# The third norm and the routing on the scaled residual: where a token's factor is put

## What is computed

```python
x = x + jnp.einsum('bsd,de->bse', merged, w_out[l])
h = rms_norm(x, g_ffn[l])          # x * rsqrt(mean(x*x, -1) + EPS) * g_ffn
...
logits = jnp.einsum('bsd,de->bse', h, w_router)
top_val, top_idx = lax.top_k(logits, TOP_K)
top_w = jax.nn.softmax(top_val, axis=-1)
for e in range(N_EXPERTS):
    out = out + gates[..., e:e + 1] * swiglu(h, w1[e], w3[e], w2[e])
```

## Time and profile before

| | us |
|---|---|
| time, median of 3 runs | 1642.52 (1641.66 to 1648.16) |
| profiled execution, its time | 1649.6 |
| profiled execution, its span | 1647.8 |
| PE busy | 1613.0 (98%) |
| DVE busy | 1280.3 (78%) |
| ACT busy | 1040.6 (63%) |

### The profile page before, as it was taken

One profiled execution on the slowest core, in us unless ns is written; L12 is line 12 of the kernel. 1 busy time (PEld: TensorE's weight loads), 2 busy tenths in 40 slices (PEclk: granted clock), 3 DMA queues, 4 the chain that ended last, 5 costly groups with the idle time before them and its releaser, 6 DMA issues.

```text
span 1647.8 us, 23908 instructions
## 1 busy us (share of the span) xinstructions
PE 1613.0 (98%) x9544; PEld 1420.8 (86%) x9544; DVE 1280.3 (78%) x1103; ACT 1040.6 (63%) x914; POOL 15.6 (1%) x16
## 2 busy tenths in 40 slices
PE   7999989999899998999999999999999999999998
PEld 6999989999899997888888888888888888888887
DVE  5985763445697566987988987987987987987986
ACT  5545443544554625777777777777777777777774
POOL 0000100000000010000000000000000000000000
PEclk9999999999999997999999999999999999999999
DMA  8543545555354451999999999999999999999994
GB/s 291 166 150 131 173 133 182 180 194 187 124 159 145 137 179 60 366 367 338 366 367 339 365 366 338 365 365 338 366 366 338 365 366 338 365 366 339 364 366 177
DMA packets 182147, 452.56 MB, mean 275 GB/s; under 512 B 6992, under 2 KB 80720, under 8 KB 181968
## 3 DMA queue, kind: packets, MB, share of 16 engines
q1 hardware_dynamic: 182096, 451.82, 76.3%
HBM read 450.74 MB, written 1.05 MB: 274 GB/s over the span
## 4 chain that ended last, share of the span: by engine, by line
PE 97%; DVE 2%; ACT 0%; issue 0%; DMA 0%; DVEq 0%; ACTq 0%
PE bank L293 30%; PE bank L294 29%; PE bank L295 29%; PE bank L1347 2%; PE bank L1368 1%; PE bank L1389 1%; PE bank L1084 1%; DVE h_full L655 1%; PE bank L1201 1%; DVE rinv L645 0%; PE bank L1192 0%; PE bank L1185 0%; PE bank L1135 0%; DVE w_low L283 0%; PE bank L1184 0%; DVE h_low L650 0%
## 5 line engine op out<-in xcount | busy, mean ns | idle before, releaser
L283 DVE TENSOR_TENSOR w_low<-raw,w_high 128x2048 fp32r<-128x2048 f32 x427 | 959.0, 2292 | 129.3 <-ACT w_high L279 129.0
L279 ACT ACTIVATE w_high<-raw 128x2048 fp32r<-128x2048 f32 x427 | 803.3, 1918 | 134.1 <-DMA raw<-exp_w 132.2
L293 PE MATMUL bank<-w_high,hg_high 128*128 128x512 f32 x896 | 352.9, 394 | 0.7 <-issue 0.7
L294 PE MATMUL bank<-w_low,hg_high 128*128 128x512 f32 x896 | 350.1, 391 | 0.0
L295 PE MATMUL bank<-w_high,hg_low 128*128 128x512 f32 x896 | 350.0, 391 | 0.0
L293 PE MATMUL bank<-h_high,w_high 128*128 128x256 f32 x1056 | 301.9, 286 | 5.6 <-DVE h_low L650 4.8
L295 PE MATMUL bank<-h_high,w_low 128*128 128x256 f32 x1056 | 295.5, 280 | 0.0
L294 PE MATMUL bank<-h_low,w_high 128*128 128x256 f32 x1056 | 295.5, 280 | 0.0
L293 PEld LDWEIGHTS bank<-h_high,w_high 128*128 128x128 f32 x1056 | 201.1, 190 | 12.3 <-issue 10.7
L294 PEld LDWEIGHTS bank<-h_low,w_high 128*128 128x128 f32 x1056 | 199.8, 189 | 1.6 <-issue 1.4
L293 PEld LDWEIGHTS bank<-w_high,hg_high 128*128 128x128 f32 x896 | 168.9, 189 | 36.0 <-issue 0.9
(11 more groups left out here) (250 smaller groups left out, 1525.9 us busy)
## 6 DMA issues: line engine op xcount, KB each, us to landing
raw<-exp_w SPq DMA_DIRECT2D x336, 1024.0 KB, 5.1
raw<-w_in SPq DMA_DIRECT2D x42, 1024.0 KB, 5.2
raw<-ffn_w SPq DMA_DIRECT2D x33, 1024.0 KB, 5.3
raw<-w_out SPq DMA_DIRECT2D x8, 1024.0 KB, 5.0
raw<-w_br_attn SPq DMA_DIRECT2D x4, 1024.0 KB, 5.1
raw<-w_br_pool SPq DMA_DIRECT2D x2, 1024.0 KB, 4.7
raw<-w_br_conv SPq DMA_DIRECT2D x2, 1024.0 KB, 5.5
cst<-consts SPq DMA_DIRECT2D x1, 1280.0 KB, 13.5
```

What stands on the lines that cost most here:

```text
L279: nc.scalar.activation(wh[c % RING][:], raw[c % RING][:], ACT.Copy).then_inc(s["high_done"], 1)
L283: nc.vector.tensor_tensor(wl[c % RING][:], raw[c % RING][:], wh[c % RING][:].bitcast(F32), ALU.subtract).then_inc(s["split_done"], 1)
L293: pe.matmul(dst, lh, rh, start=start and i == 0, stop=False)
L294: pe.matmul(dst, lh, rl, start=False, stop=False)
```

## The change

Only the norm ahead of the experts is changed, in layer 1. The residual is scaled by g_ffn alone, without the norm's factor, as its blocks become ready: ACT writes the high part `y_high`, squares x, and writes a full copy to `gate` (`x_scaled`); DVE writes the low part `y_low` (`x_scaled_low`). The router's logits are made from these, PE turns the full copy into rows by token, and the factor of a token, now one number in its partition, is put on the logits and on the rows as they are copied out (`scale=rtok`). The sum of squares is made for it with a single column of ones (`token_sums`, L1377), so that it lands by token in a partition. Three splits of expert weights on ACT and DVE move from the routing into the four steps of the residual, three clearing writes move from DVE to GpSimd, and the exponential moves behind the four `gather_out`. The core of the diff:

```diff
             def experts():   # ScalarE, and in mixer() ahead of it
-                squares(2 * l + 1, 0)
-                squares(2 * l + 1, 1)
...
+                else:
+                    for m in range(4):
+                        x_scaled(m)
+                        if m < 3:
+                            split_high(act, MOE0 + m)
...
+            def x_scaled(m):
+                x_ready(act, 3, m)
+                for k in (2 * m, 2 * m + 1):
+                    ins = nc.scalar.activation(yH[:, k, :], xT[:, k, :], ACT.Copy, scale=A(1, A_GFFN + k))
+                ins.then_inc(s["xg_high"], 1)
+                squares(3, m)
+                for k in (2 * m, 2 * m + 1):
+                    ins = nc.scalar.activation(xgf[:, k, :], xT[:, k, :], ACT.Copy, scale=A(1, A_GFFN + k))
+                ins.then_inc(s["xg_full"], 1)
...
-                norm(3)
-                split_high(act, MOE0)
-                split_high(act, MOE0 + 1)
...
+                act.wait_ge(s["norm_stats"], 4)
+                for t in range(TT):
+                    ins = nc.scalar.activation(root2[:, t:t + 1], bank[(3, 6)[t]][:, 0:1], ACT.Sqrt, bias=A(0, A_EPS),
+                                               scale=1.0 / D)
+                ins.then_inc(s["norm_root"], 1)
+                act.wait_ge(s["norm_step"], 4)
+                for f, (t, half_) in enumerate(GROUPS):
+                    act.wait_ge(s["xg_turned"], f + 1)
+                    nc.scalar.activation(htH[:, t, 512 * half_:512 * half_ + 512], bank[XG_BANKS[f]][:], ACT.Copy,
+                                         scale=rtok[:, t:t + 1]).then_inc(s["ht_high"], 1)
...
             # VectorE
-                residual(33)
-                residual(34)
...
+                for m in range(4):
+                    residual(33 + m)
+                    if l == 0 and m in (1, 2):
+                        split_low(dve, b + MIX_PIECES + m - 1)
+                    elif l:
+                        if m < 3:
+                            split_low(dve, MOE0 + m)
+                        x_scaled_low(m)
...
+            def ht_low(f):
+                t, half_ = GROUPS[f]
+                cols = slice(512 * half_, 512 * half_ + 512)
+                dve.wait_ge(s["ht_high"], f + 1)
+                nc.vector.scalar_tensor_tensor(out=htL[:, t, cols], in0=bank[XG_BANKS[f]][:], scalar=rtok[:, t:t + 1],
+                                               in1=htH[:, t, cols].bitcast(F32), op0=ALU.mult,
+                                               op1=ALU.subtract).then_inc(s["ht_low"], 1)
...
             # TensorE
+                def token_sums(m):
+                    pe.wait_ge(s["squares"], 12 + m + 1)
+                    for k in (2 * m, 2 * m + 1):
+                        for t in range(TT):
+                            ins = pe.matmul(bank[(3, 6)[t]][:, 0:1], hf[:, k, t * P:t * P + P], ones[:, 0:1],
+                                            start=k == 0, stop=k == KC - 1)
...
+                for k in range(6):
+                    logits(k)
+                for m in range(3):
+                    token_sums(m)
+                for f in range(2):
+                    pe.wait_ge(s["xg_full"], 2)
+                    turn_group(xgf, XG_BANKS[f], f, "xg_turned")
+                logits(6)
+                logits(7).then_inc(s["f_raw"], 1)
+                token_sums(3).then_inc(s["norm_stats"], 1)
+                for f in range(2, 4):
+                    pe.wait_ge(s["xg_full"], 4)
+                    turn_group(xgf, XG_BANKS[f], f, "xg_turned")
+                small_turn(7, 0, 3, "r_logits")
```

More of the change, by code:

```diff
@@ L537, in experts @@
             def experts():
-                norm(3)
-                split_high(act, MOE0)
-                split_high(act, MOE0 + 1)
[L541 to L551, removed]
+                act.wait_ge(s["norm_stats"], 4)
[8 more added lines that the diff above has]
+                                         scale=rtok[:, t:t + 1]).then_inc(s["ht_high"], 1)
+                for f, (t, half_) in enumerate(GROUPS):
+                    act.wait_ge(s["x_turned"], f + 1)
+                    nc.scalar.activation(xacc[:, t, 512 * half_:512 * half_ + 512], bank[X_BANKS[f]][:],
+                                         ACT.Copy).then_inc(s["x_copied"], 1)
                 def gather_out(g, count):
@@ L575, in experts @@
                     gather_out(g, 0)
+                act.wait_ge(s["r_lg"], 1)
+                nc.scalar.activation(wt[:, 1, :], wt[:, 0, :], ACT.Exp).then_inc(s["r_exp"], 1)
                 def job(j):
@@ L660, in norm, with x_scaled_low @@
                 low(3)
+            def x_scaled_low(m):
+                dve.wait_ge(s["xg_high"], m + 1)
+                for k in (2 * m, 2 * m + 1):
+                    ins = nc.vector.scalar_tensor_tensor(
+                        out=yL[:, k, :], in0=xT[:, k, :], scalar=A(1, A_GFFN + k), in1=yH[:, k, :].bitcast(F32),
+                        op0=ALU.mult, op1=ALU.subtract)
+                ins.then_inc(s["xg_low"], 1)
             def mixer(l):
@@ L1320, in experts, with logits @@
             def experts():
-                small_h(bank[7][:, S:2 * S], 64, 3)
-                for f in range(12):
-                    src = (hH, hL, xT)[f // 4]
-                    if f >= 7:
-                        pe.wait_ge(s["fill_act"], f - 6)
-                    if f == 4:
-                        small_turn(7, 0, 3, "r_logits")
-                    t, half_ = f % 4 // 2, f % 2
-                    for k in range(4):
-                        a = src[:, 4 * half_ + k, t * P:t * P + P]
-                        ins = pe.transpose(bank[f % 7][:, k * P:k * P + P], a if f >= 8 else a.bitcast(F32), ident)
-                    ins.then_inc(s["fill"], 1)
+                def logits(k):
+                    if k % 2 == 0:
+                        pe.wait_ge(s["xg_low"], k // 2 + 1)
+                    at = 64 + 8 * k
+                    return products(pe, bank[7][:, S:2 * S], [
+                        (wfH[:, at:at + P], wfL[:, at:at + P], yH[:, k, :], yL[:, k, :])], start=k == 0, stop=k == KC - 1)
@@ new lines, in token_sums, with turn_group @@
+                def token_sums(m):
+                    pe.wait_ge(s["squares"], 12 + m + 1)
+                    for k in (2 * m, 2 * m + 1):
+                        for t in range(TT):
+                            ins = pe.matmul(bank[(3, 6)[t]][:, 0:1], hf[:, k, t * P:t * P + P], ones[:, 0:1],
+                                            start=k == 0, stop=k == KC - 1)
+                    return ins
+                def turn_group(src, b, f, name):
+                    t, half_ = GROUPS[f]
+                    for k in range(4):
+                        ins = pe.transpose(bank[b][:, k * P:k * P + P], src[:, 4 * half_ + k, t * P:t * P + P], ident)
+                    ins.then_inc(s[name], 1)
@@ L1333, in experts @@
+                small_turn(7, 0, 3, "r_logits")
+                pe.wait_ge(s["norm_root"], 4)
+                for f in range(2):
+                    turn_group(xT, X_BANKS[f], f, "x_turned")
                 pe.wait_ge(s["r_pick"], 1)
```

72 lines of the change are left out of this document (42 added, 30 removed).

## The result

| | changed kernel | kernel before |
|---|---|---|
| time, median (range), us | 1651.51 (1647.75 to 1659.68), 20 runs | 1642.25 (1636.78 to 1649.19), 20 runs |
| profiled execution, its time | 1648.27 | 1649.6 |
| its span | 1646.5 | 1647.8 |
| mean granted clock in it | 0.987 | 0.988 |

The medians differ by 9.3 us. The ratio of changed to before, an estimate over all the runs and not the quotient of the two medians, is 1.0053, slower by 0.53%, with a 95% interval of 1.004 to 1.0066. The interval lies on both sides of the 0.5% that the prediction took as its bound.

The account below looks back on a forecast made before the run. PE holds 97% of the chain, and the change lies in the stretch before job 0. Residual round trips and a half-clock backlog start job 0 9.1 us later: 1642.5 + 9 = 1651.5 us, range 1641.5 to 1655.

Parts of the forecast that it names:

- The circle: Layer 1's four residuals: each waits for a round trip through ACT and DVE, 7.7 us instead of PE's 6.3.
- The clearing writes on GpSimd: At 605.7 to about 608, while DVE stands idle waiting for ACT's w_high1; costed at nothing.
- The backlog behind the last low part: PE's logits, sums and turned rows from 629.65, at half clock to 643.2; DVE takes the logits 8.1 us later.
- The one-column entry: Sums of squares on PE: 0.217 us per entry at half clock, bounds 0.11 and 0.217.
- Half clock throughout: PE from the backlog until into job 0 stays at 1.2 GHz; the forecast case, chance 0.75.
- rival 1: Clock returns in the backlog by 633, drops again before the gathers: +2.5 us, 1645; chance 0.13.
- the prediction's own sign of being wrong: PE's clock at 1.00 between 633 and 657, or a residual following its unit on PE within a microsecond.
- The exponential and the fourth split: Exponential behind the last `gather_out`: split ready at 667.8, needed by PE at 668.0, so PE waits below 1 us.
- The sum: Job 0 and all behind it move by +9.1 us; against the median, 1642.5 + 9 = 1651.5.
- Rival 2: Clock full from the backlog into job 0, PE waits for the fourth split: -1.3 us, 1641; chance 0.07.
- Rival 3: Residuals come at PE's pace, the round trip not binding; job 0 starts near 633: -15 us, 1627.5; chance 0.03.
- The size against 0.5%: Same means within 8.2 us, 1634.3 to 1650.7; chances: slower 0.53, same 0.43, faster 0.04.

Follow-up runs that it names:

- a0_same: The changed kernel run again with no edit: median 1654.38 us over 6 runs, ratio 1.0057 to the kernel before.
- a1: The changed kernel with DVE's split of each expert piece one residual later, behind that step's low parts: 1637.32 us, ratio 0.9961 to before.
- a3: The changed kernel with sums of squares and the first two groups of turned rows issued between the logits on PE: 1647.55 us, ratio 1.0022 to before.
- a6: The changed kernel with late DVE splits, exponential ahead of `gather_out`, and turned logits ahead of the last two groups of turned rows: 1629.86 us, ratio 0.9921 to before.
- a2: The changed kernel with the exponential put back ahead of the four `gather_out` on ACT: 1650.96 us, ratio 1.0033 to before.
- a5: The changed kernel with both the late DVE splits and the exponential ahead of the four `gather_out`: 1634.43 us, ratio 0.9959 to before.
- a4: The changed kernel with the exponential first and 30 plus 54 unread products filling PE's waits between logits: 1646.69 us, ratio 1.0011 to before.
- a7: The same kernel as a6, unchanged, on another occasion: 1631.8 us over 6 runs, ratio 0.9936 to before.

## Why the prediction was right, step by step

The forecast was 1651.5 us and the median is 1651.51. The agreement to 0.01 us is luck: the same kernel gives two kinds of executions some 4 us apart, each with or without 7 us of a slower dense loop, and the median falls among them; with the six runs of a0_same it is 1652.3. The circle and its size are no luck.

- **The circle.** Forecast: residuals 9.1, 7.7 and 7.7 us apart, each behind a w_low that waits for ACT's w_high. Measured: 9.04, 7.78 and 7.77, behind waits of 5.62, 4.10 and 4.09 us. Shown as the cause by a1, in which the edit of one order on DVE takes 14 us off.
- **The clearing writes on GpSimd.** They were costed at nothing, and ran from 598.55 to 601.01 in after, while DVE had no work until 604.05. No residual or low part waited for them.
- **The backlog behind the last low part.** Confirmed by a3 (shorter by what goes elsewhere, 3.7 to 5 us). The one-column entry, which no row of before showed, was taken at 0.217 us between bounds of 0.11 and 0.217, and took 0.205 at half clock: 0.012 too much each, 0.4 us over 32. One addition in the working is off by 0.15 us: eight transposes of 1.75 from 647.7 end at 649.45, not 649.3.
- **The clock.** Half clock throughout is what a0_same's profile shows, and there scaling is 0.1 us, the gathers 0.3 and job 0 0.1 us from the forecast. The first profile goes part of the way of rival 1: the clock came back within the backlog and was gone again 0.7 us into the gathers (639.9). But it came back at +35, where that rival had it at +27.7 (633 on the times of before): all 24 of the first entries ran at half clock (4.91 us), and scaling came at +36.80, 1.2 us ahead of the forecast's +37.99, where the rival had +33.1. It loses 5.8 us and not the rival's 2.5. On the times of before the clock was at 1.00 from 640.3 to 647.2, so the prediction's own sign of being wrong, a clock of 1.00 between 633 and 657, shows for 7 of these 24 us in this execution. So the step that was wrong is the weight of "I take half clock until into job 0": that is one of two common outcomes, ten of 26 by their mean clock, and was given 0.75; a return in the backlog was given 0.13, with too early a point.
- **The exponential and the fourth split.** Forecast: they fit by 0.2 us, PE waits less than 1. PE waited 0.79 us in after and 0.65 in a0_same, for the clock came back 3.6 and 3.9 us into job 0, where the sum had 6.1, so that PE was through with its 36 products sooner. That a sooner start would be worth less for it was right too: 2.50 us in a1.
- **The sum.** +9.1 was forecast for job 0 and all behind it; +9.15 at the combine in a0_same, +5.8 in after. Set against the before executions that most of its runs are like (about 1642), the times of the two kinds without the slower dense loop, 1648 and 1651.4 to 1654.4, are 6 and 9.5 to 12.5 more; a0_same's has 2 us more ahead of the changed stretch too (600.00 against 598.01).
- **The rivals.** Rival 2 (full clock throughout) and rival 3 (no circle) did not occur. Rival 3 as a mechanism is a1 and a6: with the circle taken out the kernel is faster than before, by 5 to 13 us, less than the 15 of the rival. The last low part was ready at +17.0 in both (614.47 + 0.88 in a1), where the rival had +14.8; the clock fell in the backlog all the same; and in a1 PE waited for the fourth split.
- **The size against 0.5%.** 9.3 us against the bound of 8.2, with an interval on both sides of it: as close as the chances 0.43 and 0.53 had it.

What stays open: why the clock returns 35 us behind residual 33 in one execution and only at +55 in another, with the same instructions in front of it. The Trainium skill ("TensorE: Matmul & The Clock Gate", Part 1: The HAM clock gate) says that the number of slow matmuls at a start differs from run to run of one kernel; the two profiles of the same kernel agree. Open too is what the exponential's place is worth in time (a2, a5), and why the dense loop has two paces.

## What to carry to other kernels

Where an engine works its stream in order, add up the whole trip round two engines before work is put into the gaps of a step: 5.4 us of it under a pace of 6.3 left the time of this kernel as it was, 7.8 us turned a gain of 5 us into a loss of 9. A split that feeds something much later belongs behind the instructions for which the other engine waits, one step late; that single order turned 0.5% slower into 0.4% faster. And PE's waits were paid twice here, in themselves and in the low clock behind them (3.6 us in a4). Price such a backlog at half clock: even with work at full rate right up to it, the clock fell within it in a1 and a4 to a7.

## What the runs showed of the hardware

Two things about TensorE's clock, and one about the dense loop. First, the clock fell while PE had no wait at all. In a1 PE was busy for all of 614 to 618 us (windows), in products of 256 columns until 613, then one-column sums (613.08 to 615.8) and eight turned blocks:

```profile
614.00:616.00 2.00, 2.00 (x20) 2.00 (x20) 0.99 (x4) 1.76 (x5) 0.00 (x0) 1.00 0.76 313
616.00:618.00 2.00, 2.00 (x12) 2.00 (x11) 0.00 (x0) 0.00 (x0) 0.00 (x0) 0.54 0.00 0
```

The same in a4, behind 10 us of busy products, a wait of 0.3 us and the same sums:

```profile
626.00:628.00 2.00, 2.00 (x16) 2.00 (x17) 0.00 (x0) 0.00 (x0) 0.00 (x0) 0.78 0.00 0
```

It also fell so in a5 (0.62 over 616 to 617, then 0.50), a6 (622 to 624: 0.92, then 0.50) and a7 (614 to 616: 1.00, then 0.50). In before it held through the turned rows of 631.3 to 637 and the rank's start, behind logits, so turned rows alone are not enough to explain it; the five kernels in which it fell so have the 24 one-column entries just ahead. Whether these are the cause was not tried by itself. A one-column float32 matmul costs two entries of 0.114 us at full clock and 0.205 at half, 4.91 us for the 24 entries of twelve matmuls that give one number per token.

Second, being busy did not bring the clock back. In a0_same PE was busy without a break from 625 to 639.8 us, in logits, one-column sums and turned rows, and the granted clock was 0.50 in all of it; in before it returned at 630.0, behind logits that ran one behind the other from 626.70.

The last is the dense loop's two paces, 172 and 179 matmuls in 20 us at a granted clock of 1.00 in both and with no wait of PE in either: 7 us of the time of an execution, nearly as much as the change itself.
